# First projection group among the opening modulation loads, keys group first in layer 1

## The reference

```python
for l in range(DEPTH):                                   # DEPTH = 2
    shift, scale, gate = jnp.split(sc @ w_ada[l] + b_ada[l], 3, axis=-1)      # sc = silu(c), w_ada[l]: 2048 x 6144
    shift_c, scale_c, gate_c = jnp.split(scc @ w_ada[l] + b_ada[l], 3, axis=-1)
    h = rms(x, norm_w[l]) * (1.0 + scale[:, None]) + shift[:, None]
    hc = rms(xc, norm_w[l]) * (1.0 + scale_c) + shift_c
    qa, ka, va, qb, kb, vb, qc, kc, vc, z = project_stream(h, *weights, rope=(cos, sin))   # h @ w_in[l], 6208 columns
    qa_c, ka_c, va_c, qb_c, kb_c, vb_c, qc_c, kc_c, vc_c, z_c = project_stream(hc, *weights, rope=None)
    ...
    x = x + gate[:, None] * merge_out(o_a, o_b, o_c, z, w_out[l])
    ...
```

## Time and profile before

| | |
|---|---|
| median of three runs | 3440.72 us (3440.68 to 3442.89) |
| the profiled execution | 3442.21 us, span 3440.9 us |
| TensorE busy | 3286.7 us, 96% of the span |
| VectorE busy | 1652.0 us, 48% |
| ScalarE busy | 1359.9 us, 40% |
| GpSimd busy | 172.5 us, 5% |
| mean granted clock of TensorE | 0.982 |
| read from HBM | 550.10 MB |

### The profile page before, as it was taken

The page is one execution under the profiler, slowest core; times in us unless marked ns, Lnnn a source line. Parts: engine busy times, 40 slices in busy tenths (PEclk is TensorE's granted clock), DMA queues, the critical chain, the costliest instruction groups (busy, mean ns, idle before and its releaser), DMA issues.

```text
span 3440.9 us, 52141 instructions
## 1 busy us (share of the span) xinstructions
PE 3286.7 (96%) x21958; PEld 2853.5 (83%) x21958; DVE 1652.0 (48%) x2682; ACT 1359.9 (40%) x2179; POOL 172.5 (5%) x252
## 2 busy tenths in 40 slices
PE   6899999988999989999799999999999999999998
PEld 1588888873448889888459999999999999999998
DVE  0422233374563363444575675555555645454444
ACT  1422232343443253434454443334444444444343
POOL 2000000001001101000201000000000000000000
PEclk9999999998999999999899999999999999999999
DMA  9533222226654254433435455555555555555554
GB/s 341 193 120 125 92 93 97 80 78 232 229 201 147 98 177 154 145 125 109 156 137 182 158 180 184 186 183 188 188 186 187 169 185 189 185 188 186 188 186 153
DMA packets 152826, 566.09 MB, mean 165 GB/s; under 512 B 17520, under 2 KB 17648, under 8 KB 151440
## 3 DMA queue, kind: packets, MB, share of 16 engines
q1 hardware_dynamic: 146160, 529.52, 45.6%
q0 software_dynamic: 6432, 33.23, 2.7%
HBM read 550.10 MB, written 12.58 MB: 164 GB/s over the span
## 4 chain that ended last, share of the span: by engine, by line
PE 89%; DMA 5%; DVE 3%; ACT 2%; issue 1%; POOL 0%; SPq 0%; DVEq 0%; ACTq 0%; POOLq 0%
PE ps L702 20%; PE ps L704 20%; PE ps L703 19%; PE ps L691 7%; PE ps L693 7%; PE ps L692 7%; DMA sb_raw<-in_stream 5%; PE ps L617 2%; PE ps L824 1%; PE ps L810 1%; PE ps L787 1%; PE ps L803 1%; PE ps L778 1%; DVE sb_wlo L1249 1%; PE ps L735 1%
## 5 line engine op out<-in xcount | busy, mean ns | idle before, releaser
L1249 DVE TENSOR_TENSOR sb_wlo<-sb_raw,sb_whi 128x1024 fp32r<-128x1024 f32 (+1 forms) x814 | 992.2, 1220 | 1323.1 <-ACT sb_whi L899 1322.0
L899 ACT ACTIVATE sb_whi<-sb_raw 128x1024 fp32r<-128x1024 f32 (+1 forms) x818 | 860.0, 1052 | 1124.0 <-PE ps L704 887.6
L702 PE MATMUL ps<-sb_hn_hi,sb_whi 128*128 128x256 f32 (+4 forms) x2944 | 829.9, 282 | 4.1 <-DVE sb_hn_lo L1317 4.1
L703 PE MATMUL ps<-sb_hn_lo,sb_whi 128*128 128x256 f32 (+4 forms) x2944 | 828.8, 282 | 0.0
L704 PE MATMUL ps<-sb_hn_hi,sb_wlo 128*128 128x256 f32 (+4 forms) x2944 | 827.9, 281 | 0.0
L702 PEld LDWEIGHTS ps<-sb_hn_hi,sb_whi 128*128 128x128 f32 x2944 | 556.7, 189 | 5.1 <-DVE sb_hn_lo L1317 4.4
L704 PEld LDWEIGHTS ps<-sb_hn_hi,sb_wlo 128*128 128x128 f32 x2944 | 556.8, 189 | 0.0
L703 PEld LDWEIGHTS ps<-sb_hn_lo,sb_whi 128*128 128x128 f32 x2944 | 556.7, 189 | 0.0
L693 PE MATMUL ps<-sb_whi,sb_lo 128*128 128x512 f32 (+1 forms) x968 | 373.9, 386 | 0.0
L702 PE MATMUL ps<-sb_hi,sb_whi 128*128 128x512 f32 (+1 forms) x1024 | 347.5, 339 | 14.6 <-DVE sb_lo L1297 14.6
L691 PE MATMUL ps<-sb_whi,sb_hi 128*128 128x512 f32 x896 | 353.6, 395 | 0.0
(11 more groups left out here) (265 smaller groups left out, 4002.0 us busy)
## 6 DMA issues: line engine op xcount, KB each, us to landing
sb_raw<-in_stream SPq DMA_DIRECT2D x992, 512.0 KB, 3.4
sb_raw<-in_stream SPq DMA_DIRECT2D x18, 384.0 KB, 3.0
sb_T<-in_x POOLq DMA_DIRECT2D x1, 4096.0 KB, 16.4
z_scratch<-sb_scr POOLq DMA_DIRECT2D x16, 256.0 KB, 2.5
sb_zb<-z_scratch POOLq DMA_DIRECT2D x16, 256.0 KB, 3.0
sb_bias<-in_bias POOLq DMA_DIRECT2D x4, 1024.0 KB, 10.5
x_scratch<-sb_T POOLq DMA_DIRECT2D x1, 4096.0 KB, 11.5
sb_T<-in_x POOLq DMA_DIRECT2D x2, 1536.0 KB, 7.7
```

Of the source, the lines that this page charges most:

```text
L702: PE.matmul(o, whi[:, s, w], xh, start=k == 0, stop=False)
L703: PE.matmul(o, whi[:, s, w], xl, start=False, stop=False)
L899: AC.activation(whi[:, s, 0:width], raw[:, r, 0:width], ACT.Copy).then_inc(*hi.up((g.id, c)))
L1249: VE.tensor_tensor(wlo[:, s, 0:width], raw[:, r, 0:width], whi[:, s, 0:width].bitcast(F32), ALU.subtract).then_inc(*lo.up((g.id, c)))
```

## The change

- The modulation groups of layer 0 are computed in the order shift 0, scale 0, shift 1, scale 1, ... (`ADA_ORDER`), and `layer_scale` makes the factor for four feature blocks as soon as a pair is there (step `scale`). The copy of the row becomes a step of its own (`ada_row`).
- The 16 squares of x move into groups 0 and 1, and mean, root and broadcast into group 2.
- z group 0 of layer 0 is interleaved: its input blocks 0 to 3 are made during group 2, 4 to 7 during group 4, 8 to 11 during group 6, 12 to 15 after group 7; its chunks 0 and 1 run in group 3, 2 and 3 in group 5, 4 in group 7 and 5 to 7 after it. With the lead of two, seven projection loads come before the last modulation load.
- Group 20 leaves the attention of layer 1 (`ADA_PACE`): chunks 0 to 3 go between the last four squares of layer 0's result, 4 to 7 behind the broadcast; it uses PSUM bank 4 (`ADA_BETWEEN`), and its turn comes after the second projection chunk.
- In layer 1 `ckv` is the first group instead of z 0, and is the one whose input is made as it runs.

```diff
-ADA_PACE = ([8, 0] + [4, 2, 2, 0] * 11, [8, 0] + [2, 2, 2, 2, 0, 0] * 3)
+ADA_ORDER = [0, 4, 1, 5, 2, 6, 3, 7] + list(range(8, 24))
+ADA_BETWEEN = 20
+ADA_PACE = ([8, 0] + [4, 2, 2, 0] * 11, [8, 0] + [2, 2, 2, 2, 0, 0] * 2)
...
+    if l:
+        first.insert(0, first.pop(5))
...
-                    made = upto
+                    made = max(made, upto)
...
-    for g in range(ADA_FIRST):
+    opening = layers[0][0]
+    chunks = pl.chunks(opening, DT)
+    for i in range(ADA_FIRST):
         for c in range(8):
-            pl.ada(g, c)
-            if c == 3 and g:
-                pl.add("ada_turn", g - 1)
-            if c % 4 == 3:
-                pl.add("square", "x", (g * 8 + c) // 4)
-    pl.add("mean", "x")
+            pl.ada(i, c)
+            if c == 7:
+                pl.add("ada_row", i)
+            if i < 2:
+                pl.add("square", "x", 8 * i + c)
+            if i == 2 and c == 2:
+                pl.add("mean", "x")
+                pl.add("layer", 0)
+            if c == 3 and i:
+                pl.add("ada_turn", i - 1)
+                if i % 2 == 0:
+                    pl.add("scale", 0, i // 2 - 1)
+            if c >= 4 and i and i % 2 == 0:
+                pl.add("make", opening[0], 2 * i - 4 + c - 4)
+            if i % 2 and i > 1 and (c == 1 or c == 5 and i < 7):
+                next(chunks)
     pl.add("ada_turn", ADA_FIRST - 1)
-    for _ in range(LEAD):
-        pl.split()
+    pl.add("scale", 0, 3)
+    for k in range(12, DT):
+        pl.add("make", opening[0], k)
+    for _ in chunks:
+        pass
...
-        pl.add("layer", l)
-        pl.gemm(first)
+        if l:
+            pl.add("layer", l)
+            ada_some(4)
+            pl.add("scale", l, None)
+            chunks = pl.chunks(first)
+            next(chunks)
+            pl.add("ada_row", ADA_BETWEEN)
+            next(chunks)
+            pl.add("ada_turn", ADA_BETWEEN)
+            for _ in chunks:
+                pass
...
+        if l == 0:
+            for n, p in zip((2, 1, 1, 0), pl.pending):
+                pl.add("evac", *p)
+                ada_some(n)
+            pl.pending = []
         pl.flush()
...
     def ada_bank(g):
-        return 6 + g % 2 if g < ADA_FIRST else 7
+        return 6 + g % 2 if g < ADA_FIRST else 4 if g == ADA_BETWEEN else 7
...
+            if c == 0 and g == ADA_BETWEEN:
+                PE.wait_ge(*v_ev.at("x", 0, 12))
...
+            if g is pl.groups[1]:
+                PE.wait_ge(*v_ev.at("ada", ADA_FIRST - 1))
+                PE.wait_ge(*v_ev.at("rstd", "x"))
+            if g.before is layer_last[0]:
+                PE.wait_ge(*v_ev.at("ada", ADA_BETWEEN))
...
-        def layer_scale(l):
-            nw = param[:, PARAM["norm_w"][0] + DT * l:PARAM["norm_w"][0] + DT * (l + 1)]
-            VE.wait_ge(*v_ev.at("ada", 7 if l == 0 else 19))
+        def layer_scale(l, pair):
+
+            VE.wait_ge(*v_ev.at("ada", 2 * pair + 1 if l == 0 else 19))
+            ks = slice(4 * pair, 4 * pair + 4) if l == 0 else slice(0, DT)
+            m, n = 48 * l + DT, PARAM["norm_w"][0] + DT * l
...
-            rstd("x" if l == 0 else 0, SC[:, 0, :])
+            VE.wait_ge(*v_ev.last())
```

45 lines of the change are left out of this document (24 added, 21 removed).

## The result

| | before | after |
|---|---|---|
| median | 3441.8 us (3440.68 to 3444.0, 4 runs) | 3419.91 us (3417.34 to 3425.93, 4 runs) |
| the profiled execution | 3442.21 us, span 3440.9 | 3425.93 us, span 3424.6 |
| TensorE busy, mean granted clock | 3286.7 us, 0.982 | 3291.0 us, 0.976 |

The ratio is 0.9944 (95% interval 0.9931 to 0.9956). The medians are 22 us apart, the ratio gives 19 (15 to 24), where 41 were forecast, and the time lies above the range of 3390 to 3418. The profiled execution is the longest of the four; what follows explains the 16.3 us by which its span is shorter.

The account below looks back on a forecast made before the run. TensorE, 96% busy, was taken to bound the kernel, with gains only where it idles, runs slow or sheds work. 3442.2 less 28.0, 7.5 and 5.0 gives 3401.7; the median lies 1.5 lower, so 3400 us, range 3390 to 3418.

Parts of the forecast that it names:

- The attention of layer 1: Attention of layer 1: without group 20 its time falls out whole, gain 5.0 us, bounds 0 to 5.
- Keys group first: Start of layer 1: the 10.4 us lost to makers and low clock come back, less 1.05 for group 20's turn.
- The delay between the layers: Before layer 1: group 20's chunks delay the first projection matmul by 1.9 us, bounds 0 to 4.
- service behind the store: Between the layers: loads served behind the store of x make the first projection matmul 3.9 us late, the upper bound.
- The opening: Start of layer 0: interleaving z group 0 with the modulation loads gains 28.0 us, bounds 22.5 and 32.
- the stream therefore still sets the pace: Opening: TensorE's 53 to 74 us of work fits below 72 us of loads, so the loads set the pace.
- 0.8 us per chunk: Opening: stall charged for each of five interleaved projection chunks, between 0 and 1.9 us, 4.0 us in all.
- the ring stalls more: Rival for the opening: each interleaved chunk stops the stream for most of its 5.44 us; about 3427 us, chance 0.17.
- The clock fell: Rival for the opening: TensorE gets 1.2 GHz through the interleaved stage, slower than before, about 3452 us; chance 0.05.
- Mean, root and broadcast: Opening: they lie inside group 2, where TensorE waits for loads anyway; squares 1.27 us each, done near 45 us.

Follow-up runs that it names:

- e4: Changed kernel, but the store of x is issued only after the last chunk of modulation group 20; 3418.16 us, ratio 0.9926 against the kernel before.
- e5: Changed kernel with eight raw blocks instead of four for the first 68 loads; 3402.95 us, ratio 0.9889 against the kernel before.
- e1: Kernel before with only the change's opening, layer 1 as before; 3429.63 us, ratio 0.9959 against the kernel before.
- e3: Changed kernel with group 20 back in the attention of layer 1, keys group still first; 3427.66 us, ratio 0.9953 against the kernel before.
- e11: Changed kernel with eight raw blocks in the opening and group 20 back in the attention of layer 1; 3409.06 us, ratio 0.9889 against the kernel before.
- e12: Changed kernel with eight raw blocks, earlier mean and first splits, group 20 back in layer 1's attention; 3397.31 us, ratio 0.9866 against the kernel before.
- e8: Changed kernel with eight raw blocks in the opening and the store of x behind group 20; 3402.68 us, ratio 0.9886 against the kernel before.
- e6: Changed kernel, four blocks, with the five interleaved projection chunks one in each of groups 3 to 7; 3413.18 us, ratio 0.9922 against the kernel before.
- e7: Kernel before with eight raw blocks instead of four for the opening's 64 loads; 3417.71 us, ratio 0.9936 against the kernel before.
- e9: Changed kernel, four blocks, squares before rotary factors on GpSimd and first two projection blocks split earlier; 3428.4 us, ratio 0.9945 against the kernel before.
- e10: Changed kernel with squares and first splits earlier, eight raw blocks, store of x behind group 20; 3397.32 us, ratio 0.9861 against the kernel before.

## Why the prediction was wrong

**The attention of layer 1: right.** Forecast 5.0. The distance to the kernel before grows from 10.05 us at the first modulation chunk of that attention (1686.24 to 1676.19) to 15.2 at its value matmuls (1814.01 to 1798.82): 5.1.

**Keys group first: the number right, in part by luck.** Forecast 10.4 less 1.05 for the turn, 9.35. From the first projection matmul to the first modulation chunk of the attention it is 462.79 us before, 453.75 after, 453.17 in e4 and 453.64 in e5, and 462.81 in e1, which has z 0 first: 9.0 to 9.6. But e3, e11 and e12, which have the keys group first and nothing of group 20 there, took 454.73 to 455.92 us: the move alone gives 6.9 to 8.1, not 10.4. The makers' share of the loss is gone (TensorE is busy for 50.00 of the first 50 us, 43.62 before); the low clock is not: it is 0.95 in these 50 us in e3 and e12, 0.94 in e11, as before (0.96), against 0.99 in the changed kernel and 1.00 in e4. The forecast let the low clock go with the makers' loss. In the changed kernel, where TensorE works on group 20 up to the first projection matmul, it went too; that the one is the reason for the other was not tried by itself.

**The delay between the layers: the term was mis-sized, 10.0 for 1.9, outside its own bounds of 0 to 4.** Two causes. 5.7 us remain in e4, and its timeline puts 5.4 of them ahead of the broadcast, where the four modulation chunks stand among the means. I took them at the full clock and partly hidden; the clock is 0.50 in the window from 1205 us, as at the end of this hole before, and each modulation chunk (1.92) and each mean (1.87) then stands in full in the chain to the root. The other 4.3 are the store of x, shown by e4 (3.6 by e8 against e5). I had made service behind the store the upper bound (3.9 us) and had taken none of it; I had not added the two costs up, and together they lie outside the bounds. By the Trainium skill, "DMA: Bandwidth & Descriptors", section "Queues, rings and completion order", each engine takes turns between its queues packet by packet; I read that as equal shares, 3 us for a load. The trace doesn't contradict the turns: a packet of the store is 29 KB (4.19 MB in 144) and one of the weights 3.75 KB (1.43 MB in 381), so that turns needn't mean equal bytes. Measured: a quarter of the bytes, and 11.0 us a load. That the sizes of the packets are the reason was not tested.

**The opening: the step that failed is "the stream therefore still sets the pace", with its 0.8 us per chunk.** Forecast: 47 loads at 1.54 us and 4.0 us of stalls, row 7 at 131.2, gain 28.0. Measured: row 7 at 146.79, gain 10.5 (14.0 in e1). The last modulation chunk was to come 14.8 us later than before and came 30.4 later. Five chunks at 5.44 us are 27.2, so the moved work was added, not hidden. The change gained in the opening only what the old hole behind row 7 had cost, less what it brought along: the way from row 7 to z end shrank by 40.9 us, 27.2 of them the moved chunks and 13.7 the hole, and row 7 moved by 30.4. The 15.6 us between 131.2 and 146.79 are 5.3 by the copy of row 2 (60.23 for 54.95) and 10.3 in the stretch behind it; behind row 7 it was 1.9 more than the 18.0 of the forecast, 1.6 of which e1 doesn't have (19.35 us from row 7 to z end, 20.95 in the changed kernel). What made the sum wrong:

- *The pace was the ring's, not the DMA's, and TensorE had no time to spare.* I read 0.95 as a full DMA. But with four blocks a load is issued only when TensorE has used one, so time that TensorE spends on a chunk is soon time in which the stream stands, and TensorE pays for it with waits behind the chunk. I had the needs of TensorE (53 to 74 us) and of the stream (72) nearly equal and took the larger of the two plus 4.0; the stretch took 72.2 us of TensorE and 14.3 of waits. TensorE's need was at the upper end: the modulation chunks took 35.1 us where I had 20 to 42, and the projection chunks and turns 37.1 where I had 32.5, in part at the lower clock. The stall was also bounded from the wrong row: 3.4 us from issue to landing is the median of the whole kernel; in the opening it was 5.1 with four in flight, and 4.2 to 6.1 in the chain of the changed kernel. My rival "the ring stalls more" had this mechanism and 3427 us, at a chance of 0.17; the result lies between the two. e6 shows that the nearness of the chunks is not a cause of any size. e5 and e7 show that the four blocks are not all of it: with eight row 7 is 14.3 us earlier, but in the kernel before it is 15.5 earlier, and interleaving still adds 31.5.
- *The clock fell.* I gave it 0.05, on the ground that it was 1.00 with TensorE at 73%. In the changed kernel it is 0.67 and 0.56 in two windows, and falls behind waits of 1.9 and 2.0 us. The Trainium skill, "TensorE: Matmul & The Clock Gate", section "HAM oscillation", tells of a clock that falls again at waits for a DMA; the opening before had spoken against it, with 33 waits for single loads from row 2 to row 7, none longer than 1.22 us, at a clock of 1.00. This stage, with eight such waits, six of them of 1.3 to 2.0 us, agrees with it. But the length of the stretch doesn't follow the clock: e1 and e4, with the same opening, had 0.90 and 0.87 where the changed kernel had 0.80, and their stretches took 84.67 and 88.84 us against 86.56. So the rival's mechanism appeared, in some two fifths of the stretch, but with half as much of it (e1) the stretch was only 1.9 us shorter.
- *Mean, root and broadcast were not free in group 2.* The fifteen adds of the squares took 1.40 us each, not 1.27, and the mean waits for them; the first splits stand behind the first makes (3.36 us of idle at 64.52). With four blocks the repair gains nothing (e9), because the early splits hold two of them; with eight it is 10 us (e10 against e8).

The runs show that the two repairs, more blocks and an early start, work only together, and that even with both the interleaving adds 20.8 us to row 7, not the 14.8 of the forecast; they don't give each cause a share of the 15.6 us of its own. That the clock falls because of the waits was not tried by itself.

## What to carry to other kernels

A stream that looks saturated may be bound by its buffers. That the time from issue to landing plus use, divided by the number of blocks, equals the time per load only says that the blocks are always full; run the kernel once with more blocks to see whether the stream gets faster (here they alone gained as much as the whole change). Before work is moved among loads, add up what the engine has to do there and hold it against its time, not against the stream's: where both are nearly equal and the engine is also the one that frees the blocks, the work adds instead of hiding. A hole at the low clock on the critical path is a poor place for filler ahead of its last step, least of all beside a large store. And compare the stages that the change touches before the totals: here 19 us of scatter stood in a stage that no kernel changed.

## What the runs showed of the hardware

- 512 KB loads into SBUF ran at 312 to 343 GB/s with four in flight and at 409 to 411 GB/s with eight (windows of 20 us from 20 to 100 us, in the kernel before and in e7). From 60 to 100 us the busy share of the DMA engines was 0.95 in the first case (334 and 336 GB/s) and 1.03 in the second: it hardly tells the two apart. In the prediction I drew on the Trainium skill, "DMA: Bandwidth & Descriptors", section Specifications, for a limit of about 358 GB/s from HBM. The row gives it as half of what two cores share; this kernel runs on one core, e7's windows, 409 and 410 GB/s, are above it, and the measurement decides.
- A 4 MB store beside 512 KB loads took three quarters of the bytes (4.19 of 5.62 MB in 15 us), and the loads 11.0 us each.
- Two modulation chunks of 128x32 by 512 in different strips of the array took 1.06 us together where one alone took 1.05 (85.83 in the changed kernel).
- TensorE's granted clock was 0.67 from 80 to 100 us in the changed kernel with 14.60 us of 20 busy, and 1.00 in the kernel before with 14.63 busy. The same busy share goes with either level; what differs in the timelines from row 2 to row 7 is the length of the waits for loads, 1.3 to 2.0 us for six of eight in the one, 0.2 to 0.6 us for 25 of 33 in the other.
- The middle of layer 0, with the same instructions in each kernel, took 1024 to 1043 us, with 17.5 to 26.3 us of waits for modulation loads and 31 to 55 us at the lower clock (e7 and e11).
